# Three-tap convolutions on ScalarE and VectorE, and a half boundary that moves by one token per stage, in an eight-core encoder kernel

## The reference, cut to what matters

```python
h = concat([meta, x], axis=1)
# stage m0: mixer A (GLU, depthwise conv of 31 taps, LayerNorm, silu) beside mixer B (pooling)
# stages f0 and f1:
def conv_glu(x, w_up, b_up, conv_w, conv_b, w_down, b_down):
    h = x @ w_up + b_up                        # 1024 -> 2 * 2816
    g, v = split(h, 2)
    g = dwconv(g, conv_w, conv_b)              # centred, 3 taps, per channel
    return (silu(g) * v) @ w_down + b_down
# stage m1:
def mixer_c(x, w_in, b_in, conv_w, conv_b, w_out, b_out):
    bg, cg, v = split(x @ w_in + b_in, 3)      # 3 * 1024
    return (bg * dwconv(cg * v, conv_w, conv_b)) @ w_out + b_out   # 3 taps
# after every stage: x = layer_norm(4 ** 0.25 * x + stage(x))
```

## Time and profile before

| what | us |
|---|---|
| median of 3 runs | 1847.82 (1846.91 to 2034.84) |
| the profiled execution's own time | 1847.39 |
| its span, slowest core | 1845.8 (cores: 1840.0 to 1845.8) |
| TensorE busy | 1687.4 (91%) |
| VectorE busy | 881.9 (48%) |
| ScalarE busy | 681.0 (37%) |
| GpSimd busy | 134.8 (7%) |

### The profile page before, as it was taken

The page is one execution under the profiler, slowest core; times in us unless marked ns, Lnnn a source line. Parts: engine busy times, 40 slices in busy tenths (PEclk is TensorE's granted clock), DMA queues, the critical chain, the costliest instruction groups (busy, mean ns, idle before and its releaser), DMA issues.

```text
span 1845.8 us, 30958 instructions; the slowest of 8 cores (1840.0 to 1845.8 us)
## 1 busy us (share of the span) xinstructions
PE 1687.4 (91%) x12252; PEld 1119.8 (61%) x12252; DVE 881.9 (48%) x2269; ACT 681.0 (37%) x1288; POOL 134.8 (7%) x200
## 2 busy tenths in 40 slices
PE   3999798299999999999999999999999999999971
PEld 2666565156666666666656666566666666666640
DVE  1436685746632136632127746746642126632137
ACT  1326344526543026543014424426543025433020
POOL 3000000010000000000000000000000000000000
PEclk9999999599999999999999999999999999999995
DMA  9902310063333343334434344333344444442412
GB/s 143 233 15 47 57 24 1 1 103 60 57 59 58 63 71 58 58 60 72 66 59 68 57 66 66 54 58 59 58 69 69 68 67 88 90 90 40 63 16 92
DMA packets 72523, 120.04 MB, mean 65 GB/s; under 512 B 3392, under 2 KB 36416, under 8 KB 72384
## 3 DMA queue, kind: packets, MB, share of 16 engines
q0 software_dynamic: 59616, 100.87, 34.6%
q1 hardware_dynamic: 12768, 17.20, 3.2%
HBM read 210.53 MB, written 8.39 MB: 119 GB/s over the span
## 4 chain that ended last, share of the span: by engine, by line
PE 85%; DVE 8%; ACT 3%; DMA 2%; issue 1%; POOL 1%; DVEq 0%; ACTq 0%; POOLq 0%
PE ps L477 45%; PE ps L1056 17%; PE ps L484 6%; PE ps L1021 6%; PE ps L875 6%; DMA ringA<-wA 2%; PE ps L560 2%; PE ps L558 2%; PE ps L902 1%; DVE ps L574 1%; DVE hr L589 1%; DVE hr L585 1%; PE ps L1130 1%; DVE zz L520 1%; DVE arena L489 0%
## 5 line engine op out<-in xcount | busy, mean ns | idle before, releaser
L477 PE MATMUL ps<-hb,ringA 128*128 128x344 bf16 (+3 forms) x5952 | 945.7, 311 | 36.1 <-DMA ringA<-wA 30.6
L477 PEld LDWEIGHTS ps<-hb,ringA 128*128 128x128 bf16 x5952 | 571.3, 98 | 324.6 <-issue 43.2
L1056 PE MATMUL ps<-arena,ringB 128*128 128x344 bf16 x2112 | 308.6, 309 | 0.0
L1028 DVE SCALAR_TENSOR_TENSOR arena<-ps,PT,tf 128x344 bf16<-128x344 f32 x264 | 151.4, 575 | 324.3 <-ACT tf L1025 324.0
L1056 PEld LDWEIGHTS ps<-arena,ringB 128*128 128x128 bf16 x2112 | 206.6, 98 | 101.4
L1007 ACT ACTIVATE gbuf<-ps,PT 128x346 bf16<-128x346 f32 (+1 forms) x264 | 145.3, 550 | 203.1 <-PE ps L477 123.2
L1025 ACT ACTIVATE tf<-ps,PT 128x344 f32<-128x344 f32 x264 | 143.9, 546 | 168.0 <-PE ps L1021 167.8
L421 POOL DMA_DIRECT2D ringA<-wA x140 | 98.6, 705 | 1242.7 <-PE ps L1021 664.2
L1060 DVE TENSOR_TENSOR hr<-ps,hr 128x344 f32<-128x344 f32 x96 | 49.6, 517 | 255.5 <-PE ps L1056 255.5
L518 ACT ACTIVATE zz<-hr 128x344 bf16<-128x344 f32 x184 | 80.0, 480 | 239.4 <-DVE hr L1060 201.3
L1021 PE MATMUL ps<-gbuf,diag 128*128 128x344 bf16 x792 | 158.1, 309 | 0.0
(11 more groups left out here) (106 smaller groups left out, 996.0 us busy)
## 6 DMA issues: line engine op xcount, KB each, us to landing
ringA<-wA POOLq DMA_DIRECT2D x140, 512.0 KB, 5.3
ringB<-wB POOLq DMA_DIRECT2D x32, 704.0 KB, 6.8
hr<-xT SPq DMA_DIRECT2D x6, 1376.0 KB, 26.7
outT<-hr SPq DMA_DIRECT2D x5, 1376.0 KB, 7.3
hb<-xT POOLq DMA_DIRECT2D x8, 261.8 KB, 12.0
hb<-xT POOLq DMA_DIRECT2D x8, 254.2 KB, 24.5
outT<-hr SPq DMA_DIRECT2D x1, 1312.0 KB, 9.1
PT<-pt SPq DMA_DIRECT2D x1, 284.0 KB, 3.0
```

The costliest lines, as they stand in the source:

```text
L477: inst = pe.matmul(bk[:, o0:o1], wslot[:, kc, c0:c0 + 128], src[:, kc, sa:sbnd], start=(kc == 0), stop=(kc == 7))
L1028: S.op("dve", lambda e: e.scalar_tensor_tensor(out=hid[:, j, a - lo:a - lo + TT], in0=bV[:, 0:TT], scalar=pcol("ffn_b_up", l * 44 + 22 + j ...
L1056: inst = pe.matmul(bk[:, 0:TT], wslot[:, kc, :], hid[:, kc, a - lo:a - lo + TT], start=(kc == 0), stop=(kc == NFC - 1))
```

## The change

The boundary between the halves is no longer 1032 in all stages, but 1032, 1031, 1030 and 1029 for m0, f0, m1 and f1 (`CUT`). Half 0 of a stage then reads nothing beyond what half 0 of the stage before has written, and the one gate column that half 1 needs from half 0 is kept in `gsave` (copies on GpSimd). `mini_ln`, `hnext`, `hsave` and the matmuls out of them are gone.

The three-tap convolution is made without TensorE. In the FFN, for each channel: G of three tiles into banks 0 to 2, from each of which ScalarE makes two copies, one to `gb2` (bfloat16) and one to `cb2` (float32, times the middle tap); V of three tiles into banks 3 to 5; VectorE adds the outer taps over the whole half of about 1032 tokens (`taps`, two instructions); ScalarE applies silu over the whole half; VectorE multiplies by V, tile by tile. There is one set of V banks, and a channel has six calls of `S.pe_unit()` in place of three. In m1 the order becomes two channels' products, then the two channels' B units, and the convolution is a ScalarE instruction and two taps. The steps of the LayerNorm that run beside an FFN are written after every fourth `S.pe_unit()` (`stride=4`). The DMA scratch size is set to 8192. The constants of the middle tap are made once, by four small VectorE instructions.

```diff
+TW = 348
+CUT = {"m0": 1032, "f0": 1031, "m1": 1030, "f1": 1029}
+ENDS = {"f0": 1032, "m1": 1031, "f1": 1030}
+POINTS = sorted({0, TT, 2 * TT, HT + TT, HT + 2 * TT, T} | set(CUT.values()))
+NSEG = len(POINTS) - 1
+
+def out_tiles(stage):
+    B = CUT[stage]
+    return [(0, TT), (TT, 2 * TT), (2 * TT, B), (B, HT + TT), (HT + TT, HT + 2 * TT), (HT + 2 * TT, T)]
+
+def in_tiles(stage):
+    B = ENDS[stage]
+    t = out_tiles(stage)
+    return t[:2] + [(2 * TT, B)] + t[3:]
+
+def segs(a, b):
+    return [i for i in range(NSEG) if POINTS[i] < b and POINTS[i + 1] > a]
...
-    nc = bass.Bass("TRN2", target_bir_lowering=False)
+    nc = bass.Bass("TRN2", target_bir_lowering=False, dynamic_dma_scratch_size=8192)
...
-            a_order.extend(range(GA_M1IN, GA_M1IN + 12))
+            for i in range(4):
+                a_order.extend([GA_M1IN + 2 * i, GA_M1IN + 2 * i + 1, GA_M1IN + 8 + i])
...
-    def mm_hb(pe, bk, wslot, c0, a, b, use_save, use_next=False):
-        parts = []
-        if use_next:
-            assert b == HT + 1 and a < HT
-            parts.append((hb, a, HT, 0, HT - a))
-            parts.append((hnext, 0, 1, HT - a, HT - a + 1))
-        elif use_save and a < HT:
-            parts.append((hsave, a - (HT - HALO), HT - (HT - HALO), 0, HT - a))
-            parts.append((hb, HT, b, HT - a, b - a))
-        else:
-            parts.append((hb, a, b, 0, b - a))
+    def hr_keys(c, a, b):
+        return [("hr", c, i) for i in segs(a, b)]
+
+    def mm_hb(pe, bk, wslot, c0, a, b):
         inst = None
-        for (src, sa, sbnd, o0, o1) in parts:
-            for kc in range(8):
-                inst = pe.matmul(bk[:, o0:o1], wslot[:, kc, c0:c0 + 128], src[:, kc, sa:sbnd],
-                                 start=(kc == 0), stop=(kc == 7))
+        for kc in range(8):
+            inst = pe.matmul(bk[:, 0:b - a], wslot[:, kc, c0:c0 + 128], hb[:, kc, a:b],
+                             start=(kc == 0), stop=(kc == 7))
...
-    def ln_chain(items, base=1, per=13, split0=True):
+    def ln_chain(items, base=1, per=13, split0=True, stride=1):
...
-                S.defer(base + per * i + k, touched, run)
+                S.defer(base + stride * (per * i + k), touched, run)
...
-        if h == 1 and not final:
-            mini_ln(ln_idx)
-        ln_chain([main_ln_item(ln_idx, t, final) for t in tiles])
-
-    def save_halo():
-        S.op("dve", lambda e: e.tensor_copy(out=hsave[:, :, :], in_=hb[:, :, HT - HALO:HT]),
-             reads=[("hb", 2)] + [("hbc", c, 0) for c in range(NCH)], writes=["hsave"])
+        ln_chain([main_ln_item(ln_idx, t, final) for t in tiles], stride=stride)
...
-            out_proj(h, cat, GA_M0OUT, 0, final=(n_stages == 1))
+            out_proj(h, cat, GA_M0OUT, 0, final=(n_stages == 1), stride=(1 if h == 0 else 4))
...
+    def taps(buf, cb, n, w0, w2, kbuf, kcb):
+        S.op("dve", lambda e: e.scalar_tensor_tensor(out=cb[:, 0:n], in0=buf[:, 0:n], scalar=w0, in1=cb[:, 0:n],
+                                                     op0=ALU.mult, op1=ALU.add),
+             reads=kbuf + [kcb, "PT"], writes=[kcb])
...
+        cw = lambda k, j: pcol("ffn_conv_w", (l * 3 + k) * 22 + j)
...
+        for x in range(2):
+            pad = 0 if h == 0 else nh + 1
+            S.op("pool", lambda e, x=x, pad=pad: e.memset(gb2[:, x, pad:pad + 1], 0.0), writes=[("g2", x, y) for y in range(5)])
+        for j in range(NFC):
+            wslot, wk = a_group(ga0 + j)
+            x = j % 2
+            gb, cb, kcb = gb2[:, x, :], cb2[:, x, :], ("cb", x)
+            if h == 1:
+                S.op("pool", lambda e, gb=gb, j=j: e.tensor_copy(out=gb[:, 0:1], in_=gsave[:, j:j + 1]),
+                     reads=[("gsave", j)], writes=[("g2", x, 3)])
+            for i in range(3):
+                (a, b), (oa, ob) = itl[i], otl[i]
+                n, no = b - a, ob - oa
+                S.op("pe", lambda pe, i=i, a=a, b=b, wslot=wslot: mm_hb(pe, ps[i], wslot, 0, a, b),
+                     reads=[wk] + hb_keys(a, b), writes=[("ps", i)])
+                S.op("act", lambda e, i=i, a=a, n=n, j=j, gb=gb: e.activation(
+                    out=gb[:, a - lo + 1:a - lo + 1 + n], in_=ps[i][:, 0:n], func=AF.Identity,
+                    bias=pcol("ffn_b_up", l * 44 + j), scale=1.0),
+                    reads=[("ps", i), "PT"], writes=[("g2", x, i)])
+                S.op("act", lambda e, i=i, oa=oa, no=no, j=j, cb=cb: e.activation(
+                    out=cb[:, oa - lo:oa - lo + no], in_=ps[i][:, 0:no], func=AF.Identity,
+                    bias=dcol("w1b", l * 22 + j), scale=cw(1, j)),
+                    reads=[("ps", i), "PT", "DT"], writes=[kcb])
+                S.pe_unit()
+            taps(gb, cb, nh, cw(0, j), cw(2, j), [("g2", x, y) for y in range(5)], kcb)
+            if h == 0:
+                S.op("pool", lambda e, gb=gb, j=j: e.tensor_copy(out=gsave[:, j:j + 1], in_=gb[:, nh:nh + 1]),
+                     reads=[("g2", x, 2)], writes=[("gsave", j)])
+            for i in range(3):
+                a, b = otl[i]
+                S.op("pe", lambda pe, i=i, a=a, b=b, wslot=wslot: mm_hb(pe, ps[3 + i], wslot, 128, a, b),
+                     reads=[wk] + hb_keys(a, b), writes=[("ps", 3 + i)])
+                if i == 1:
+                    S.op("act", lambda e, cb=cb, j=j: e.activation(out=cb[:, 0:nh], in_=cb[:, 0:nh], func=AF.Silu),
+                         reads=[kcb], writes=[kcb])
+                S.pe_unit()
+            for i in range(3):
+                a, b = otl[i]
+                n = b - a
+                S.op("dve", lambda e, i=i, a=a, n=n, j=j, cb=cb: e.scalar_tensor_tensor(
+                    out=hid[:, j, a - lo:a - lo + n], in0=ps[3 + i][:, 0:n],
+                    scalar=pcol("ffn_b_up", l * 44 + 22 + j), in1=cb[:, a - lo:a - lo + n],
+                    op0=ALU.add, op1=ALU.mult),
+                    reads=[("ps", 3 + i), kcb, "PT"], writes=[("hid", j, tiles[i])])
...
-            ln_chain([main_ln_item(2 * l + 1, t, final) for t in tiles])
+            ln_chain([main_ln_item(2 * l + 1, t, final) for t in tiles], stride=(4 if h == 0 else 1))
...
+            x = j % 2
+            cb, kcb = cb2[:, x, :], ("cb", x)
+            kcv = [("cv", j, y) for y in (0, 1, 2, "pad")]
+            S.op("act", lambda e: e.activation(out=cb[:, 0:nh], in_=cvb[:, j, 1:nh + 1], func=AF.Identity,
+                                               bias=pcol("conv_c_b", j), scale=pcol("conv_c_w", 8 + j)),
+                 reads=kcv + ["PT"], writes=[kcb])
+            taps(cvb[:, j, :], cb, nh, pcol("conv_c_w", j), pcol("conv_c_w", 16 + j), kcv, kcb)
...
+        def b_unit(j, jl, wslot, wk):
+            x = j % 2
+            cb, kcb = cb2[:, x, :], ("cb", x)
+            for i, t in enumerate(tiles):
+                a, b = otl[i]
+                n = b - a
+                bB, kB = bank()
+
+                def one(bB=bB, kB=kB, a=a, b=b, n=n, t=t):
+                    S.op("pe", lambda pe: mm_hb(pe, bB, wslot, jl * 128, a, b), reads=[wk] + hb_keys(a, b), writes=[kB])
+                    S.op("dve", lambda e: e.scalar_tensor_tensor(
+                        out=ybuf[:, j, a - lo:a - lo + n], in0=bB[:, 0:n], scalar=pcol("b_in_c", j), in1=cb[:, a - lo:a - lo + n],
+                        op0=ALU.add, op1=ALU.mult),
...
+            for jl in range(2):
+                wslot, wk = a_group(GA_M1IN + 2 * ii + jl)
+                cv_unit(2 * ii + jl, wslot, wk)
             wslot, wk = a_group(GA_M1IN + 8 + ii)
             for jl in range(2):
-                j = 2 * ii + jl
-                if j + 1 < 8:
-                    build_cdiag(j + 1)
-                for t in tiles:
-                    a, b = t * TT, (t + 1) * TT
-                    bB, kB = bank()
-                    S.op("pe", lambda pe, bB=bB, a=a, b=b, wslot=wslot, jl=jl: mm_hb(pe, bB, wslot, jl * 128, a, b, False),
-                         reads=[wk] + hb_keys(a, b), writes=[kB])
-                    bC, kC = bank()
-
-                    def conv(pe, bC=bC, j=j, a=a):
-                        inst = None
-                        for k in range(3):
-                            c0 = a - lo + k
-                            inst = pe.matmul(bC[:, 0:TT], diag[:, (j % 2) * 3 + k, :], cvb[:, j, c0:c0 + TT],
-                                             start=(k == 0), stop=(k == 2))
-                        return inst
-                    S.op("pe", conv, reads=[("fd", j % 2)] + [("cv", j, x) for x in (0, 1, 2, "pad")], writes=[kC])
-                    cs, kcs = tfslot()
-                    S.op("act", lambda e, bC=bC, cs=cs, j=j: e.activation(out=cs[:, 0:TT], in_=bC[:, 0:TT], func=AF.Identity,
-                                                                          bias=pcol("conv_c_b", j), scale=1.0),
-                         reads=[kC, "PT"], writes=[kcs])
-                    S.op("dve", lambda e, bB=bB, cs=cs, j=j, a=a: e.scalar_tensor_tensor(
```

(10 more changed lines are left out.)

315 lines of the change are left out of this document (105 added, 210 removed).

## The result

The changed kernel takes 1792.4 us (median; 1790.2 to 1795.1) against 1847.4 for the one before: ratio 0.9705, 95% interval 0.9686 to 0.9724. It is faster by 55 us. Forecast were 128 us, and the time lies outside the range of 1670 to 1785. The profiled execution took 1792.0 us.

What follows compares the result with a forecast made beforehand. TensorE was taken to bound the kernel and to stay the bound, with small waits for banks. From 1847.4 us, 106 (FFN), 20 (m1) and 2 (m0's one-column groups) came off: 1719 us, range 1670 to 1785.

Steps and rivals of the forecast that it cites:

- The removed matmuls and prices: TensorE loses diagonal matmuls (116 + 21 us) and one-column groups (30 us); a tap costs 1.22 us, copies 0.55 and 0.66.
- The turnaround of the V banks: FFN channel: V's banks are free 5.74 us after V starts, against 7.01 until wanted, 1.27 to spare.
- LayerNorm steps, 7 us a half: FFN: LayerNorm steps falling into the V banks' slack cost 7 us of waiting a half.
- 1.1 us, which fits: FFN: a LayerNorm step after G2 holds up the taps by 0.66 + 0.46 us, within the slack.
- The start wait: Start of an FFN half: sums of squares follow 8 matmuls, not 16, so a 0.25 us wait becomes 1.4.
- The end wait: End of an FFN up part: TensorE waits 3.3 us for the last channel's products; before, nothing.
- The slower clock behind it: After the wait before the down part: possibly a slower clock, 1 to 2 us more a half, only in the range.
- m1: m1 half: TensorE 91.1 us, stall 7, before `out_proj` 2, start 3, together 103 us; saving 20.
- 2 (all hidden): FFN and m1: no stall by LayerNorm steps (28 and 20 us), time 1671 us; chance 0.17.
- 3: FFN: V-bank turnaround carrying each channel's whole LayerNorm share becomes the bound, 8.3 us a channel, time 1808; chance 0.15.
- 4 (half-rate tap): VectorE's tap runs at half rate, 2.1 to 2.3 us, time 1900 us or more; chance 0.04.
- 5: Weight loads come late through the smaller DMA scratch: 98 us of TensorE waiting, time 1817; chance 0.04.

Runs made afterwards that it cites:

- e8: The changed kernel with the FFN's convolution back on TensorE as diagonal matmuls, LayerNorm steps at every call, moving boundary and m1 kept: 1819.8 us.
- e3: The changed kernel with one LayerNorm step per FFN channel, after V's first tile, and one per unit of the down part: 1717.1 us.
- e9: e3 with the LayerNorm steps beside m1 spread at every 1.6 calls over the half and its `out_proj`: 1695.9 us.
- e10: The changed kernel without GpSimd's 88 one-column boundary copies, the neighbour read as zero: 1788.1 us.
- e11: The changed kernel with the DMA scratch size cut from 8192 to 4096: 1794.9 us.
- e12: e9 with the first three groups of each down part made in two pieces, the last channel's block after the other 21: 1678.2 us.

## Why the prediction was wrong

The removed matmuls and prices. **Right in the main.** One-column groups cost 0.16 to 0.21 us each and not 0.25 (e8); the FFN's sum is built from what stays and did not use that price. TensorE busy 159.0 in e3's up part, where 22 x 7.01 and the sums of two tiles, 4.7, make 158.9; copies and silu within 4%, the tap 6% longer.

"No engine exceeds TensorE, but little is left." Right as busy time (VectorE 129 of 190 us), and of no help: the loop is made of two engines, each idle while the other works.

**The turnaround of the V banks: this step failed.** It put "copies 0.55 + 0.66" behind the last G, as if ScalarE had made the other four by then. In the timeline V starts at 1586.21, when ScalarE has begun the second of six; the taps start 2.68 us after V, not 1.41. The missing 1.27 us is as long as the whole slack that I saw. Of the 73 us that the time missed, 33 are waits of V beyond the 28 forecast. The reason is the order of ScalarE's program, silu before the next channel's copies, which I read but did not close into a loop: I followed one channel from TensorE and back, never from ScalarE to ScalarE.

**LayerNorm steps, 7 us a half: fell with it.** They were weighed against a slack of 1.27 that was 0. TensorE's waits for products in the up parts are 61.1 / 4 = 15.3 us a half for the 7: some 22 x 0.16 = 3.5 by the bare round, the rest by the steps in it, the table loads among them, which had no price. With the steps moved (e3) an up part is 164.2 for 185.8. The "1.1 us, which fits" behind G2 is the 1.07 us of the timeline, in full.

The start wait: 1.4 us forecast, 1.6 to 1.7 measured. The end wait: 3.3 forecast, 14.6 / 4 = 3.65 measured. The slower clock behind it, "1 to 2 us more a half, kept for the range", was real: down parts 2.8, 2.8, 1.9 and 0.6 us longer, at a granted clock of 0.97, 0.97, 0.98 and 1.00, and f0's up parts had a granted clock of 0.98 and TensorE busy for 166.2 and 167.3 us, f1's 1.00 and 163.3 and 164.0, where the sum had 161.2. So of the 16 us of busy time that were missed, about 6 came with the slower clock. The rest is about 2.5 us an up part at the full clock; my estimate of it is that each of some 14 waits ends a dense group, whose last matmul counts with 0.31 us in place of 0.146, 14 x 0.16 = 2.2. Neither stood in the sum.

**m1**: idle 12.5 us of 108.1, forecast 12 (7 + 2 + 3), and by the mechanism named (e9). What was missed is TensorE's busy time, 95.6 for 91.1: by my estimate the granted clock of 0.98 makes 91.1 / 0.98 = 93.0 of it, and the ends of dense groups at 14 waits, by the estimate above, 2.2 more.

GpSimd's copies at 0: right within the 4 us of e10. DMA scratch at 0: right as far as it shows, for the step from 8192 to 4096 did nothing (e11) and the waits for weights are those of before (30.9 for 30.6 us); the step from the unset size to 8192 was not undone by itself. The tail is 2.2 us longer; its stores land 11.6 us (median of three), 15.6, 13.5 and 7.9 us after issue, where before it was 7.3 (median of five) and 9.1. In the other kernels it lasts 63 to 69 us. What sets it stays open.

**The rivals.** 2 (all hidden) fell, though e12 comes within 7 us of its 1671. 3 named the right sort of event, a turnaround that carries the LayerNorm, at a chance of 0.15; its price of 8.3 us a channel is near the 8.15 measured as the mean of two channels with copies, but partly by luck: its base was too short (5.74 for 7.17) and it laid the LayerNorm's whole share on the chain. By the base of 7.17 the round passes TensorE's 7.01 before any step is in it. 4 (half-rate tap): the tap is longer by 0.07, not 0.61. 5 fell. The range ended too low because it took the 5.74 as known; a chain with 1.27 of 7.01 to spare, assembled from seven durations and six hand-overs, was not known to that.
